# Expert hidden activations turned by VectorE instead of TensorE, with gate and up columns dealt to the column groups in runs

## What is computed

```python
def swiglu(h, wg, wu, wd):
    return (jax.nn.silu(h @ wg) * (h @ wu)) @ wd

def moe(h, w_router, wg, wu, wd):
    logits = (h @ w_router).astype(jnp.float32)
    top_v, top_i = lax.top_k(logits, TOP_K)
    wts = jax.nn.softmax(top_v, axis=-1)
    gate = jnp.sum(jax.nn.one_hot(top_i, N_EXPERTS, dtype=jnp.float32) * wts[..., None], axis=-2)
    acc = jnp.zeros(h.shape, jnp.float32)
    for e in range(N_EXPERTS):
        acc = acc + gate[..., e, None] * swiglu(h, wg[e], wu[e], wd[e])
    return acc.astype(h.dtype)
```

## Time and profile before

| | |
|---|---|
| Time, three runs | 1456.92, 1457.15 (median), 1460.52 us |
| The profiled execution | 1455.41 us; its span 1453.6 us |
| Granted TensorE clock | 0.997 |
| PE busy | 1420.2 us (98% of the span), 14154 matmul instructions |
| DVE, ACT busy | 306.8 us (21%), 182.8 us (13%) |
| DMA | 475.60 MB, mean 327 GB/s |
| Chain that ended last | PE 92%, DMA 4%, DVE 2% |
| Costliest lines | L1231 520.9 us, L1301 259.8 us, L784 202.6 us |

### The profile page before, as it was taken

How to read it: one execution, slowest core, us unless ns; L and a number is a source line. 1 busy time by engine, 2 the same in 40 slices (tenths; PEclk the granted TensorE clock), 3 DMA queues, 4 the chain that set the end, 5 groups by cost and what they waited for, 6 DMA issues and landing times.

```text
span 1453.6 us, 31951 instructions
## 1 busy us (share of the span) xinstructions
PE 1420.2 (98%) x14154; PEld 831.3 (57%) x14154; DVE 306.8 (21%) x748; ACT 182.8 (13%) x458; POOL 38.3 (3%) x57
## 2 busy tenths in 40 slices
PE   9999999999999999999998999999998999999997
PEld 7887887888876568335443345335443345336444
DVE  5122223224247963100010110000100110000101
ACT  3000000001024742000100000000100000000201
POOL 3000000001000001000000000000000000000000
PEclk9999999999999999999999999999999999999999
DMA  9967774446353795899999999999999999999994
GB/s 323 357 278 267 261 260 168 156 169 208 118 184 116 225 284 211 343 372 381 425 411 424 426 409 424 424 358 388 424 408 425 425 407 425 424 348 419 422 425 162
DMA packets 95121, 475.60 MB, mean 327 GB/s; under 512 B 9944, under 2 KB 35720, under 8 KB 70143
## 3 DMA queue, kind: packets, MB, share of 16 engines
q1 hardware_dynamic: 92855, 467.57, 81.9%
q0 software_dynamic: 2128, 5.99, 1.3%
HBM read 469.65 MB, written 12.71 MB: 332 GB/s over the span
## 4 chain that ended last, share of the span: by engine, by line
PE 92%; DMA 4%; DVE 2%; ACT 0%; issue 0%; SPq 0%; DVEq 0%; ACTq 0%
PE banks L1231 35%; PE banks L1301 15%; PE banks L784 14%; PE banks L802 7%; PE banks L851 5%; DMA ring<-in_w_moe_gate 4%; PE banks L1158 2%; PE banks L1343 2%; PE banks L935 1%; PE banks L765 1%; PE banks L1241 1%; PE banks L994 1%; PE banks L1085 1%; PE banks L1009 1%; PE banks L1025 1%; PE banks L952 1%
## 5 line engine op out<-in xcount | busy, mean ns | idle before, releaser
L1231 PE MATMUL banks<-ring,arena 128*32 128x512 f32 (+1 forms) x5376 | 520.9, 540 | 3.4 <-DMA ring<-in_w_moe_gate 3.4
L1231 PEld LDWEIGHTS banks<-ring,arena 128*32 128x32 f32 x5376 | 177.7, 110 | 315.7 <-issue 307.3
L1301 PE MATMUL banks<-ring,arena 128*32 128x256 f32 x4704 | 259.8, 380 | 10.2 <-DMA ring<-in_w_moe_down 6.5
L1301 PEld LDWEIGHTS banks<-ring,arena 128*32 128x32 f32 x4704 | 152.9, 110 | 109.8 <-DMA ring<-in_w_moe_down 10.4
L784 PE MATMUL banks<-hT,ring 128*128 128x264 f32 x896 | 202.6, 387 | 0.0
L784 PEld LDWEIGHTS banks<-hT,ring 128*128 128x128 f32 x896 | 169.3, 190 | 36.9 <-issue 8.4
L2133 DVE TENSOR_TENSOR xT<-banks,xT 128x264 f32<-128x264 f32 x56 | 24.2, 433 | 484.6 <-PE banks L1343 484.6
L802 PE MATMUL banks<-arena,ring 128*128 128x264 f32 x448 | 101.5, 387 | 0.0
L802 PEld LDWEIGHTS banks<-arena,ring 128*128 128x128 f32 x448 | 84.6, 190 | 19.2 <-issue 5.0
L851 PE MATMUL banks<-hT,ring 128*128 128x264 f32 x256 | 57.4, 386 | 0.0
L2153 DVE TENSOR_TENSOR arena<-arena,banks 128x512 f32<-128x512 f32 (+1 forms) x42 | 24.2, 618 | 149.0 <-PE banks L1231 149.0
(11 more groups left out here) (338 smaller groups left out, 837.1 us busy)
## 6 DMA issues: line engine op xcount, KB each, us to landing
ring<-in_w_moe_gate SPq DMA_DIRECT2D x64, 1792.0 KB, 16.1
ring<-in_w_moe_up SPq DMA_DIRECT2D x64, 1792.0 KB, 15.8
ring<-in_w_moe_down SPq DMA_DIRECT2D x32, 2048.0 KB, 20.3
ring<-in_w_moe_down SPq DMA_DIRECT2D x32, 1536.0 KB, 20.4
arena<-in_cache_kv SPq DMA_DIRECT2D x64, 256.0 KB, 8.1
ring<-in_cache_kv SPq DMA_DIRECT2D x128, 128.0 KB, 2.1
ring<-in_w_ffn_gate SPq DMA_DIRECT2D x7, 2048.0 KB, 7.9
ring<-in_w_ffn_up SPq DMA_DIRECT2D x7, 2048.0 KB, 13.4
```

Of the source, the lines that this page charges most:

```text
L1231: last = mm(banks[CT * q:CT * (q + 1), 2 * t + part, 0:PART_W[part]], xe[:, c, CT * t:CT * (t + 1)], w[:, at:at + PART_W[part]], start=(c ...
L1301: last = mm(banks[CT * q:CT * (q + 1), 6 + place // 2, 256 * (place % 2):256 * (place % 2 + 1)], mh[:, t, at:at + CT], w[:, r, 256 * h:256 ...
```

## The change

- PE's transposes and ACT's copies of them are gone (`turn_hidden`, `mt_ps`, L1241, L1546).
- DVE turns `msg` into `mh` itself, in blocks of 32x32 inside each group of 32 partitions: one STREAM_TRANSPOSE per tile and part, reading every fourth word (part 0) or third word (part 1) of `msg`.
- So that blocks suffice, hidden units must lie on the partition group where the down weights want them. Group q of `products` now takes, from each of the four 512-column (384-column) quarters of a part, the q-th run of 128 (96) columns. The streamed operand is four runs per matmul in place of one; count and sizes of the matmuls are as before.
- DVE's order: for each tile the product and the turn of part 0; then the products of part 1 of all tiles; then the turns of part 1. `mhid` and `mt_sb` count twice per tile.
- PE waits for two turned parts before down step 0, for the third inside that step (three tiles), and for all of them before step 2.
- In item 7 the small products of the final norm leave steps 0 and 1: two sets follow step 2, one each steps 3 and 4, two step 5.

```diff
+        def turned_before(i):
+
+            if isinstance(i, int):
+                return 2 * sum(ITEM_TILES[:i])
+            return i * (2 * LT) + 2 * (sum(ITEM_TILES[:LOOP0]) - LOOP0 * LT)
...
                 for part in range(2):
                     for q in range(4):
-                        at = PART_AT[part] + PART_W[part] * q
+                        cols = w[:, PART_AT[part]:PART_AT[part] + 4 * PART_W[part]]
                         last = mm(banks[CT * q:CT * (q + 1), 2 * t + part, 0:PART_W[part]], xe[:, c, CT * t:CT * (t + 1)],
-                                  w[:, at:at + PART_W[part]], start=(c == 0), stop=(c == NC - 1), skip_group_check=True)
+                                  cols.rearrange("p (j s e) -> p s j e", j=4, s=4)[:, q], start=(c == 0), stop=(c == NC - 1),
+                                  skip_group_check=True)
                 return last
 
-            def turn_hidden(i, t):
-
-                pe.wait_ge(mhid, tiles_before(i) + (t + 1))
-                for part in range(2):
-                    for r in range(PART_R[part]):
-                        a = PART_W[0] * part
-                        last = tr(banks[:, 2 * t + part, P * r:P * (r + 1)],
-                                  msg[:, t, a + r:a + PART_W[part]:PART_R[part]], ident)
-                last.then_inc(mt_ps, 1)
...
-                        if c == NC - 1 and t == 1 and nt == 3:
-                            turn_hidden(i, 0)
...
-                        at = PART_W[0] * part + P * r + CT * q4
+                        at = PART_W[0] * part + CT * (PART_R[part] * q4 + r)
...
             def down_stage(i, nt, after):
 
-                for t in range(nt):
-                    if t or nt == 2:
-                        turn_hidden(i, t)
...
-                pe.wait_ge(mt_sb, tiles_before(i) + 2)
+                pe.wait_ge(mt_sb, turned_before(i) + 2)
                 for k in range(NK):
                     wait_expert_tile(pe, i, DOWN, k)
                     if k == 0 and nt == 3:
                         down_products(k, nt, (0, 2))
-                        pe.wait_ge(mt_sb, tiles_before(i) + 3)
+                        pe.wait_ge(mt_sb, turned_before(i) + 3)
                         last = down_products(k, nt, (2, 3))
                     else:
+                        if k == 2:
+                            pe.wait_ge(mt_sb, turned_before(i) + 2 * nt)
                         last = down_products(k, nt, (0, nt))
...
-                    if not isinstance(i, int) and k < 6:
-                        if k == 5:
-                            pe.wait_ge(xe_sb, i * 2 + 4)
-                        rows_of_x(k)
+                    if not isinstance(i, int) and 2 <= k < 6:
+                        for w in ((0, 1), (2,), (3,), (4, 5))[k - 2]:
+                            if w == 5:
+                                pe.wait_ge(xe_sb, i * 2 + 4)
+                            rows_of_x(w)
...
-                for t in range(nt):
-                    act.wait_ge(mt_ps, tiles_before(i) + (t + 1))
-                    for part in range(2):
-                        a = PART_W[0] * part
-                        last = nc.scalar.copy(mh[:, t, a:a + PART_W[part]], banks[:, 2 * t + part, 0:PART_W[part]])
-                    last.then_inc(mt_sb, 1)
...
+                def hidden(t, part):
+                    a, w = PART_W[0] * part, PART_W[part]
+                    tt(msg[:, t, a:a + w], msg[:, t, a:a + w], banks[:, 2 * t + part, 0:w], ALU.mult).then_inc(mhid, 1)
+
+                def turn(t, part, n):
+                    a, w = PART_W[0] * part, PART_W[part]
+                    dve.wait_ge(mhid, turned_before(i) + n)
+                    V.transpose(mh[:, t, a:a + w].rearrange("p (j r s) -> p j r s", j=4, s=CT),
+                                msg[:, t, a:a + w].rearrange("p (j f r) -> p j r f", j=4, f=CT)).then_inc(mt_sb, 1)
+
                 for t in range(nt):
                     dve.wait_ge(msilu, tiles_before(i) + (t + 1))
...
-                    for part in range(2):
-                        a = PART_W[0] * part
-                        last = tt(msg[:, t, a:a + PART_W[part]], msg[:, t, a:a + PART_W[part]],
-                                  banks[:, 2 * t + part, 0:PART_W[part]], ALU.mult)
-                    last.then_inc(mhid, 1)
+                    hidden(t, 0)
+                    turn(t, 0, t + 1)
+                for t in range(nt):
+                    hidden(t, 1)
+                for t in range(nt):
+                    turn(t, 1, nt + t + 1)
```

More of the change, by code:

```diff
@@ L356, in build @@
             "xn_ps", "xn_act", "xn_dve", "lg_ps", "top_gap", "top_exp", "sel_ready", "pos_ps", "table_ready"))
-        P_ready, G_ready, xe_ps, xe_sb, tile_used, mgu_ps, msilu, mhid, mt_ps, mt_sb = (sem(n) for n in (
-            "P_ready", "G_ready", "xe_ps", "xe_sb", "tile_used", "mgu_ps", "msilu", "mhid", "mt_ps", "mt_sb"))
+        P_ready, G_ready, xe_ps, xe_sb, tile_used, mgu_ps, msilu, mhid, mt_sb = (sem(n) for n in (
+            "P_ready", "G_ready", "xe_ps", "xe_sb", "tile_used", "mgu_ps", "msilu", "mhid", "mt_sb"))
         gt_ps, gt_sb, yn_sb, so_ps, so_added, yt_ps, y_ready, y_stored = (sem(n) for n in (
@@ L435, in moe_source @@
             rows = w[PART_AT[part]:PART_AT[part] + 4 * PART_W[part]]
-            return rows.rearrange("(q p r) n -> p q (r n)", q=4, r=PART_R[part])[:, q]
+            return rows.rearrange("(j p r) n -> p j (r n)", j=4, r=PART_R[part])[:, q]
         def part_value(p):
@@ L1229, in products @@
                     for q in range(4):
-                        at = PART_AT[part] + PART_W[part] * q
+                        cols = w[:, PART_AT[part]:PART_AT[part] + 4 * PART_W[part]]
                         last = mm(banks[CT * q:CT * (q + 1), 2 * t + part, 0:PART_W[part]], xe[:, c, CT * t:CT * (t + 1)],
-                                  w[:, at:at + PART_W[part]], start=(c == 0), stop=(c == NC - 1), skip_group_check=True)
-                return last
-            def turn_hidden(i, t):
-                pe.wait_ge(mhid, tiles_before(i) + (t + 1))
-                for part in range(2):
-                    for r in range(PART_R[part]):
-                        a = PART_W[0] * part
-                        last = tr(banks[:, 2 * t + part, P * r:P * (r + 1)],
-                                  msg[:, t, a + r:a + PART_W[part]:PART_R[part]], ident)
-                last.then_inc(mt_ps, 1)
+                                  cols.rearrange("p (j s e) -> p s j e", j=4, s=4)[:, q], start=(c == 0), stop=(c == NC - 1),
+                                  skip_group_check=True)
+                return last
             def gate_stage(i, first, nt, before):
                 if not first:
-                    pe.wait_ge(mt_sb, tiles_before(i))
+                    pe.wait_ge(mt_sb, turned_before(i))
                 for c in range(NC):
```

## The result

| | before | with the change |
|---|---|---|
| median of five runs, us | 1457.15 (1454.75 to 1460.52) | 1443.08 (1441.52 to 1449.33) |
| ratio of the times | | 0.9903, 95% interval 0.9886 to 0.9919 |
| profiled execution, us | 1455.41 | 1449.33 |
| PE busy, DVE busy, ACT busy, us | 1420.2, 306.8, 182.8 | 1406.6, 341.8, 162.7 |

The account below looks back on a forecast made before the run. PE was taken to set the 3-tile items (0, 2, 3, 5, 6), arriving weights to end items 1 and 4. 5 x 2.8 + 1.3 = 15.3 us off, against the median 1442.0 us; range 1437 to 1453.

Parts of the forecast that it names:

- Hand-over with three tiles: From up to down products in items 0, 2, 3, 5, 6: PE starts down 2.8 us earlier per item.
- T: Time of one 512-column STREAM_TRANSPOSE on DVE, taken as 1.03 us, bounded between 0.69 and 2.0 us.
- wait for DVE: At the 3-tile hand-over: PE still stands idle 0.8 us after its last up products.
- No wait at the third tile and none at step 2: In 3-tile down stages: later turns are done before PE asks, at 660.0 against 661.7 and 665.4 against 668.7.
- Items 1 and 4, 0: 2-tile items: PE starts down 1.45 us earlier but only waits longer for weights, so 0 gained.
- The wait for weights behind the two: PE's wait for down and gate weights behind items 1 and 4 grows from 9.9 us to about 13.
- Item 7, 1.3 us: Last item, two tiles: PE starts down at 1407.7 instead of 1408.98, and the 1.3 us are kept.
- moving the small products: Norm's small products in item 7's down stage only change places within the item: 0.
- Will the DMA engines let it through: Between weight waits PE gains at most DMA idle time: 8.7 us (item 3) and 7.0 (item 6), each for 5.6 wanted.
- Runs, 0: Gate and up matmuls streaming four runs instead of one cost 0; at the end of the estimate 0.4%, about 1.6 us.

Follow-up runs that it names:

- runs only: Kernel before, with only the gate and up products streaming four runs of 128 (96) columns per matmul: 1457.71 us, ratio to before 0.9999.
- Plain read: Changed kernel, but the turn reads msg in order instead of every fourth or third word: 1442.95 us, beside 1444.51 for the change.
- first quarters: Changed kernel, DVE turning the first 128 columns of part 0 of each tile first, PE waiting for the rest before step 1: 1442.98 us, change 1443.96.
- tile order: Changed kernel, DVE doing both products then both turns per tile, PE waiting for both parts of tiles 0 and 1: 1460.66 us, ratio to before 1.0018.

## Why the prediction was right, point by point

Forecast 1442.0 us (1457.15 less 15.3 is 1441.85), measured 1443.08 (1444.5 and 1444.0 in the later series): 14.1, 13.1 and 13.5 us less than the kernel before in the same series. The mechanism and the sign hold. That the sum comes so close is partly luck: of the terms below, one was too large by 1.3 us, one too small by 0.7, and two losses, a dip and a longer item 4, were not in it.

- **Hand-over with three tiles, 2.8 us each: 2.55 us** (114.21 to 111.65, and 120.18 to 117.6, 117.78 to 115.2). The size is off by T, forecast 1.03 us and measured 1.13, two of them in the chain. T had been taken from a reduction with another step (64 words), for want of a nearer row. The wait for DVE was forecast at 0.8 us and is 0.98. No wait at the third tile and none at step 2, as expected.
- **Items 1 and 4, 0: right in kind, not quite in size.** Item 1 stays within the spread of its weights' arrival (88.0 to 88.9, before 88.35; runs only 89.14). Item 4 is 1.6 to 1.8 us longer in the three profiles of the change (89.53 to 89.69 us) than in that of before (87.92), but only 0.6 to 0.7 longer than with runs only (88.95), whose hand-over is that of before; how much of it is the change and how much the spread of the weights' arrival stays open. The wait for weights behind the two was to grow from 9.9 us to about 13; it is 10.2 to 11.3. The hand-over gained 1.28 us in item 1 (56.98 to 55.70 us after its start) instead of 1.45, and the dip behind it fills 1.7 us that would have been waiting.
- **Item 7, 1.3 us: 2.0 us without a dip, 0.3 with one.** The hand-over alone gave 1.35 (58.74 to 57.39 us after the item's start). The other 0.6 us came from moving the small products, which I had put at 0. The down stage, from its first product to the two large matmuls behind it, took 31.79 us with six interruptions by small products and takes 31.18 with four; down steps 0 to 2 run in one piece (10.57 us), and two sets in a row take 1.98 us where one took 1.11.
- **Will the DMA engines let it through: right in the result, wrong in the reckoning.** I held that PE may gain whatever the DMA engines idle over an item, 7.0 us for two 3-tile items. Plain read wanted 6.4 us and first quarters 7.0; both should just have fitted, and both gave back most of what they gained over the change (3.3 and 4.6 us in the five 3-tile items, 1.6 and 1.0 us by the medians). Their item 3 still moves 411 and 414 GB/s, below the 421 of a full stretch, so rate was left that PE's lead could not use. The kernel asks for the next tile only when PE frees its place, which is the likely reason; it was not tried by itself. Idle time over an item was an upper bound for the gain, not the gain.
- **Runs, 0: right**, by the run with runs alone (0.9999). The argument was weak, though: it rested on a weight load with a step of four words, where the stream itself takes 1.8 times as long. It came out right because a run is not a step.
- **Not in the sum: the clock.** One dip of 1.7 us on the path in each of the three profiles, behind waits of more than 2 us. It takes back nearly three times what item 7's small products gave.

Item 7's down stage, in PE's timelines: its end before the change, then its first part, the two sets in a row and its end with the change (its start before is in the earlier trace rows):

```profile
1440.77 1.13 PE L702 MATMUL banks<-cst 128*128 128x512 f32 x2
```

```profile
1403.52 10.57 PE L1296 MATMUL banks<-ring,arena 128*32 128x256 f32 x192 [2.14 <-DVE arena L2141]
1414.02 1.98 PE L1346 MATMUL banks<-cst,xT 128*88 128x128 f32 x16
1434.70 1.13 PE L708 MATMUL banks<-cst 128*128 128x512 f32 x2
```

The account of the expert stage: 5 x 2.55 + 2.0 - 1.6 - 1.7 = 11.5 us, which is 856.9 less 845.4. By the medians it is 13 to 14; the profiled execution of before was 1.7 us under its median, and runs only, with the same PE work, has 858.7 in place of 856.9; from there to 845.4 are 13.3.

## What to carry to other kernels

When an operation leaves the critical engine, write out the chain that takes its place up to the first instruction that the critical engine can start, and order it for that instruction: here the same operations in tile order, with the waits that go with it, are no faster than the kernel before, and in part order 1% faster. Before the next step on such a kernel, ask whether the second bound is already there: with weights arriving at 420 GB/s in half of the items, taking PE's remaining 4.6 us of waiting out of the 3-tile items gave 1.0 us. And look at the granted clock behind every wait of the critical engine: here waits of 2.1 to 3.15 us cost 1.7 us more in part of the cases, and cheap idle matmuls in the wait gave 1.6 us.

## What was not expected of the hardware

- STREAM_TRANSPOSE of 128x512 fp32 takes 711 ns read in order, like a copy out of PSUM (689 ns in this kernel), 1128 ns with a step of four words; of 128x384, 544 ns, and 695 ns with a step of three.
- TensorE's stream takes runs of 8 words at full rate (593 ns for a 512-column matmul in four column groups) and 1082 ns with a step of four words; 384 columns 486 ns, 687 ns with a step of three, 860 ns with four.
- Two interruptions of the column-group products by small full-width products fewer made item 7's down stage 0.61 us shorter (31.79 to 31.18), so an interruption costs some 0.3 us beyond its own products. Which part of that is the change between the two kinds was not tried.
- What sets off a clock dip behind one wait of 2.1 us and not behind another, or behind 2.80 us and not behind 2.83, stays open. With the waits of items 1, 4 and 7 filled down to 0.8 us, no dip followed them in the one profile.
